# Gate products of a linear recurrence: from fp32 to three fp32r products of split parts, two halves later, with the weights asked for by ScalarE

## The reference, cut to what matters

```
xc = causal_dwconv(xb, lru_conv_w) + lru_conv_b            # xb, xc: 256 x 2048
xh = xc.reshape(1, 256, 8, 256)                            # 8 heads of 256 channels
r  = sigmoid(einsum("bshi,hij->bshj", xh, w_a) + b_a)      # w_a, w_x: 8 x 256 x 256
i  = sigmoid(einsum("bshi,hij->bshj", xh, w_x) + b_x)
log_a = -8 * r * softplus(-lam);  a = exp(log_a)
u  = xc * i * sqrt(-expm1(2 * log_a))
h_t = a_t * h_(t-1) + u_t                                  # over the tokens
y_b = h * silu(z_b)
```

## Time and profile before

| what | value |
|---|---|
| median of three runs | 2910.55 us |
| profiled execution, its time | 2911.19 us |
| profiled execution, its span | 2909.5 us |
| TensorE busy | 2871.9 us, 99% |
| VectorE busy | 1944.8 us, 67% |
| ScalarE busy | 1644.5 us, 57% |
| mean granted TensorE clock | 0.996 |
| DMA, mean over the span | 219 GB/s |

### The profile page before, as it was taken

One profiled execution on the slowest core, in us unless ns is written; L12 is line 12 of the kernel. 1 busy time (PEld: TensorE's weight loads), 2 busy tenths in 40 slices (PEclk: granted clock), 3 DMA queues, 4 the chain that ended last, 5 costly groups with the idle time before them and its releaser, 6 DMA issues.

```text
span 2909.5 us, 40342 instructions
## 1 busy us (share of the span) xinstructions
PE 2871.9 (99%) x16476; PEld 2532.0 (87%) x16476; DVE 1944.8 (67%) x2244; ACT 1644.5 (57%) x1912; POOL 98.6 (3%) x82
## 2 busy tenths in 40 slices
PE   8999999999899999999999999999999999999998
PEld 8989988898777878788999988888899999888886
DVE  6767444535699999999675864555565678555556
ACT  6554444534478878787555544555545654444544
POOL 2212000000000000000000000000000000000000
PEclk9999999999999999999999999999999999999999
DMA  7545566645389999999555555555564545655555
GB/s 268 186 159 170 185 213 237 208 159 175 133 330 352 360 360 358 358 361 325 174 174 174 187 182 192 182 190 174 190 199 148 200 163 181 201 188 185 186 196 188
DMA packets 282102, 636.66 MB, mean 219 GB/s; under 512 B 19081, under 2 KB 32962, under 8 KB 264642
## 3 DMA queue, kind: packets, MB, share of 16 engines
q1 hardware_dynamic: 280450, 628.86, 62.8%
q10 hardware_dynamic: 1184, 4.20, 0.4%
q0 software_dynamic: 288, 1.05, 0.1%
HBM read 626.72 MB, written 7.36 MB: 218 GB/s over the span
## 4 chain that ended last, share of the span: by engine, by line
PE 92%; DVE 4%; ACT 1%; issue 1%; DMA 0%; ACTq 0%; SPq 0%; POOL 0%; DVEq 0%; POOLq 0%
PE pairs L741 16%; PE pairs L743 16%; PE pairs L742 16%; PE pairs L761 10%; PE pairs L763 10%; PE pairs L765 10%; PE pairs L1118 3%; DVE w_lo L2087 2%; PE pairs L1119 2%; PE pairs L1120 2%; PE misc L1234 2%; ACT w_hi L1478 1%; PE misc L908 1%; DVE b_lo L2606 1%; PE misc L981 0%
## 5 line engine op out<-in xcount | busy, mean ns | idle before, releaser
L2087 DVE TENSOR_TENSOR w_lo<-raw,w_hi 128x1024 fp32r<-128x1024 f32 x1072 | 1307.8, 1239 | 800.4 <-ACT w_hi L1478 793.2
L1478 ACT ACTIVATE w_hi<-raw 128x1024 fp32r<-128x1024 f32 x1072 | 1120.5, 1059 | 940.3 <-PE pairs L743 543.7
L761 PE MATMUL pairs<-a_hi,w_hi 128*128 128x256 f32 x1920 | 549.2, 286 | 2.2 <-DVE w_lo L2087 2.2
L763 PE MATMUL pairs<-a_lo,w_hi 128*128 128x256 f32 x1920 | 544.2, 283 | 0.0
L765 PE MATMUL pairs<-a_hi,w_lo 128*128 128x256 f32 x1920 | 544.1, 283 | 0.0
L741 PE MATMUL pairs<-w_hi,a_hi 128*128 128x512 f32 x1280 | 504.5, 394 | 6.0 <-DVE w_lo L2087 3.1
L743 PE MATMUL pairs<-w_hi,a_lo 128*128 128x512 f32 x1280 | 498.5, 389 | 0.0
L742 PE MATMUL pairs<-w_lo,a_hi 128*128 128x512 f32 x1280 | 498.3, 389 | 0.0
L761 PEld LDWEIGHTS pairs<-a_hi,w_hi 128*128 128x128 f32 x1920 | 369.2, 192 | 4.3 <-issue 2.4
L763 PEld LDWEIGHTS pairs<-a_lo,w_hi 128*128 128x128 f32 x1920 | 369.4, 192 | 0.5
L765 PEld LDWEIGHTS pairs<-a_hi,w_lo 128*128 128x128 f32 x1920 | 369.2, 192 | 0.0
(11 more groups left out here) (387 smaller groups left out, 3038.0 us busy)
## 6 DMA issues: line engine op xcount, KB each, us to landing
raw<-in_w_in_dram SPq DMA_DIRECT2D x232, 1024.0 KB, 5.1
raw<-in_w_out_dram SPq DMA_DIRECT2D x84, 1024.0 KB, 5.1
raw<-in_w_down_dram SPq DMA_DIRECT2D x54, 1024.0 KB, 7.1
raw<-in_w_gate_dram SPq DMA_DIRECT2D x51, 1024.0 KB, 6.0
raw<-in_w_up_dram SPq DMA_DIRECT2D x51, 1024.0 KB, 6.6
raw<-in_xattn_wk_dram SPq DMA_DIRECT2D x16, 1024.0 KB, 5.0
raw<-in_xattn_wv_dram SPq DMA_DIRECT2D x16, 1024.0 KB, 5.0
raw<-in_xattn_wq_dram SPq DMA_DIRECT2D x16, 1024.0 KB, 5.0
```

The lines of the kernel that those rows point to most:

```text
L761: nc.tensor.matmul(o, w_hi[:, s, q, fs], hi[:, k, :], start=(k == 0 and f % 2 == 0), stop=False, skip_group_check=True)
L763: nc.tensor.matmul(o, w_hi[:, s, q, fs], lo[:, k, :], start=False, stop=False, skip_group_check=True)
L1478: a.activation(w_hi[:, h % HSLOTS], landing(h)[:, 2 * (h % 2):2 * (h % 2) + 2, :], ACT.Copy).then_inc(hi_done, 1)
L2087: v.tensor_tensor(w_lo[:, h % HSLOTS], landing(h)[:, 2 * (h % 2):2 * (h % 2) + 2, :], w_hi[:, h % HSLOTS].bitcast(F32), ALU.subtract).then ...
```

## The change

The gates are computed as the large products are: `w_ax` and `xc` are split in high and low parts and three fp32r products replace each fp32 one.

- The high part of the weights, `w_ax_hi`, lies in the place of `qm` (not in use then); the low part takes the place of `w_ax` itself. The parts of `xc` go to the last quarter of `b_hi` and `b_lo`.
- ScalarE: `gate_weights_hi(j)` (two copies of 128x1024) before h6 of unit 2j+1, `conv_hi(j)` (one copy) before h4 of unit 2j+2.
- VectorE: `gate_weights_lo(l, j)` (two subtractions of 128x1024) behind h7 of unit 2j+1, `conv_lo(l, j)` (one) before h5 of unit 2j+2.
- TensorE: the blocks stand behind h3 and h4 instead of h1 and h2, 24 products each, after a wait for both low parts.
- The weights of group 0 are still asked for by SP, those of groups 1 to 3 by ScalarE right behind the sigmoids of the group before; SP's three waits go.

```diff
--- before.py
+++ after.py
@@ -274,6 +274,9 @@
         Tb = sc(9232, 4, S)
         Zb = sc(10256, 4, S)
         w_ax = sc(11280, 2, 4, S)
+        w_ax_lo = rounded("w_ax_low", 11280, [P, 2, 4, S])
+        w_ax_hi = rounded("w_ax_high", 0, [P, 2, 4, S])
+        xc_hi, xc_lo = b_hi[:, 12:16, :], b_lo[:, 12:16, :]
         w_if = sc(13328, KT, 16)
         w_if_g = w_if.rearrange("p (q r) (g c) -> p g q r c", q=4, g=2)
         vx = sc(4096, TT, 2, S + 1)
@@ -441,6 +444,8 @@
         win_done = sem("win_done")
         xp_zero = sem("xp_zero")
         vx_ones = sem("vx_ones")
+        gate_hi = sem("gate_hi")
+        gate_lo = sem("gate_lo")
         landed.append(sem("landed_fifth"))
 
         def turn_bank(n):
@@ -682,10 +687,10 @@
                 for j in range(4):
                     units(H[f"lru{l}"] + 2 * j * HALVES, 1, w_in2[l], XB2 + j * COLS)
                     for c in range(CHUNKS):
-                        if c == 1:
-
-                            if l or j:
-                                sp.wait_ge(gates_mm, 4 * l + j)
+                        if c == 1 and j == 0:
+
+                            if l:
+                                sp.wait_ge(gates_mm, 4 * l)
                             for m, name in enumerate(("w_a_2", "w_x_2")):
                                 sp.dma_start(w_ax[:, m], t[name][l, 2 * j:2 * j + 2]
                                              .rearrange("h (k p) n -> p (h k) n", p=P))\
@@ -1224,16 +1229,18 @@
             def lru_gates(l, j, a):
 
                 g = 4 * l + j
-                pe.wait_ge(conv_ok, 8 * l + j + 1)
-                pe.wait_ge(wax_in, 32 * (g + 1))
+                pe.wait_ge(gate_lo, 2 * (g + 1))
                 if g:
                     pe.wait_ge(gates_ok, g)
                 for m_ in range(2):
                     for f in range(2):
+                        o = misc[:, 2 * m_ + a, f * S:(f + 1) * S]
                         for k in range(2):
-                            m = nc.tensor.matmul(misc[:, 2 * m_ + a, f * S:(f + 1) * S],
-                                                 w_ax[:, m_, 2 * a + k, f * P:(f + 1) * P],
-                                                 xc[:, 2 * a + k, :], start=k == 0, stop=k == 1)
+                            n = 2 * a + k
+                            h, z = (w[:, m_, n, f * P:(f + 1) * P] for w in (w_ax_hi, w_ax_lo))
+                            nc.tensor.matmul(o, h, xc_hi[:, n, :], start=k == 0, stop=False)
+                            nc.tensor.matmul(o, h, xc_lo[:, n, :], start=False, stop=False)
+                            m = nc.tensor.matmul(o, z, xc_hi[:, n, :], start=False, stop=k == 1)
                 if a:
                     m.then_inc(gates_mm, 1)
 
@@ -1320,13 +1327,13 @@
                         hooks = {1: lambda: rows_out(l)}
                     if n >= 2 and n % 2 == 0:
                         j = n // 2 - 1
-                        hooks = {1: (lambda j=j: lru_gates(l, j, 0)), 2: (lambda j=j: lru_gates(l, j, 1))}
+                        hooks = {3: (lambda j=j: lru_gates(l, j, 0)), 4: (lambda j=j: lru_gates(l, j, 1))}
                     unit(pc(U[f"lru{l}"] + n), H[f"lru{l}"] + n * HALVES, n % 2, mm_features, a_hi,
                          a_lo, need=ready(4 + l) if n == 0 else {}, hooks=hooks)
                 for n in range(4):
                     hooks = {}
                     if n == 0:
-                        hooks = {1: lambda: lru_gates(l, 3, 0), 2: lambda: lru_gates(l, 3, 1)}
+                        hooks = {3: lambda: lru_gates(l, 3, 0), 4: lambda: lru_gates(l, 3, 1)}
                     unit(pc(U[f"qk{l}"] + n), H[f"qk{l}"] + n * HALVES, n % 2, mm_features, a_hi,
                          a_lo, hooks=hooks)
                 for n in range(4):
@@ -1891,6 +1898,27 @@
                                              misc[:, b + k // 2, (k % 2) * S:(k % 2 + 1) * S],
                                              ACT.Sigmoid, bias=col(f"{name}{l}", 4 * j + k))
                     m.then_inc(gates_ok, 1)
+                    if j < 3:
+                        for m, name in enumerate(("w_a_2", "w_x_2")):
+                            act.dma_start(w_ax[:, m], t[name][l, 2 * j + 2:2 * j + 4]
+                                          .rearrange("h (k p) n -> p (h k) n", p=P)).then_inc(wax_in, 16)
+
+                def gate_weights_hi(j):
+
+                    n = 4 * l + j
+                    act.wait_ge(wax_in, 32 * (n + 1))
+                    act.wait_ge(spread, 4 * GROUPS)
+                    if n:
+                        act.wait_ge(gates_mm, n)
+                    if l:
+                        act.wait_ge(bc_mm, 4 * l)
+                    a.activation(w_ax_hi[:, 0], w_ax[:, 0], ACT.Copy)
+                    a.activation(w_ax_hi[:, 1], w_ax[:, 1], ACT.Copy).then_inc(gate_hi, 1)
+
+                def conv_hi(j):
+
+                    act.wait_ge(conv_ok, 8 * l + j + 1)
+                    a.activation(xc_hi, xc, ACT.Copy).then_inc(gate_hi, 1)
 
                 def exps(j):
                     act.wait_ge(gates_ok, 4 * l + j + 1)
@@ -1917,8 +1945,11 @@
                     a.activation(dst[:, 4 * (n % 2):4 * (n % 2) + 4, :], xc, ACT.Silu)\
                      .then_inc(qk_ok, 1)
 
+                if m_ <= 7 and m_ % 2 == 1:
+                    todo[6].append(lambda: gate_weights_hi(m_ // 2))
                 if 2 <= m_ <= 8 and m_ % 2 == 0:
                     j = m_ // 2 - 1
+                    todo[4].append(lambda: conv_hi(j))
                     todo[5].append(lambda: z_silu(j))
                     todo[8].append(lambda: sigmoids(j))
                 if 3 <= m_ <= 9 and m_ % 2 == 1:
@@ -2796,6 +2827,18 @@
                 if f == 3:
                     m.then_inc(conv_ok, 1)
 
+            def gate_weights_lo(l, j):
+
+                dve.wait_ge(gate_hi, 2 * (4 * l + j) + 1)
+                for i in range(2):
+                    m = v.tensor_tensor(w_ax_lo[:, i], w_ax[:, i], w_ax_hi[:, i].bitcast(F32), ALU.subtract)
+                m.then_inc(gate_lo, 1)
+
+            def conv_lo(l, j):
+
+                dve.wait_ge(gate_hi, 2 * (4 * l + j) + 2)
+                v.tensor_tensor(xc_lo, xc, xc_hi.bitcast(F32), ALU.subtract).then_inc(gate_lo, 1)
+
             def one_minus_a2(l, j):
 
                 dve.wait_ge(a2_ok, 4 * l + j + 1)
@@ -2974,6 +3017,9 @@
                         todo[2].append(lambda i=i: conv_tile(l, i, 3))
                     if 2 <= m_ <= 8 and m_ % 2 == 0:
                         todo[3].append(lambda: z_in(l, m_ // 2 - 1))
+                        todo[5].append(lambda: conv_lo(l, m_ // 2 - 1))
+                    if m_ <= 7 and m_ % 2 == 1:
+                        todo[8].append(lambda: gate_weights_lo(l, m_ // 2))
                     if m_ == 12:
                         todo[6].append(lambda: gate_rows(l))
                     if 3 <= m_ <= 9 and m_ % 2 == 1:
```

## The result

| kernel | median us | ratio to before, 95% interval |
|---|---|---|
| before | 2911.11 (7 runs) | |
| after | 2919.89 (2919.44 to 2921.10, 7 runs) | 1.0029 (1.0020 to 1.0039) |

The change costs 8.8 us. In the profiled executions the spans stand 9.1 us apart (2918.6 against 2909.5); 0.6 of it lies before the first product of the LRU units (1365.21 against 1364.59 us), and belongs to none of the prediction's terms.

The account below looks back on a forecast made before the run. TensorE, busy 99% of the span, was taken to bound the kernel. Terms -9.1 + 4.1 + 2.7 + 14.0 + 0.4 = +12.1 us gave 2923.3 us profiled, 2922.7 us on the median; range 2906 to 2934 us.

Parts of the forecast that it names:

- The gate products: TensorE's 16 gate blocks: each takes 2.88 us as fp32r products instead of 3.45 us, -9.1 us in all.
- the old stall: TensorE's existing 0.22 us wait at h1 of odd units, once per group; its removal counted as -1.8 us.
- Stall S: h1 of odd units: later gates make TensorE wait for ScalarE behind the sigmoids, 0.73 us per group, net +4.1 us.
- The table load hidden: ScalarE's sigmoids: the 1.28 us table load runs before the wait for the gates, costing nothing; otherwise +10.2 us.
- The issues on ScalarE: Weight transfers issued behind the sigmoids, six pairs at 0.45 us: +2.7 us, with bounds 0 and +5.4.
- Stall D: Even units of groups 1 to 3: VectorE's weight subtractions make h0 to h2 late, 2.34 us six times, +14.0 us.
- The splits on ScalarE: ScalarE's high-part copies before h6 of odd and h4 of even units: hidden, no cost; uncovered, 3 us a group.
- First group: Layer 0, first group: VectorE's added subtractions make the gates start late, +0.4 us, once.
- Rival (a): TensorE never waits, decided at h2 of even units: -10.9 us, 2899.7 us; chance 0.09.

Follow-up runs that it names:

- e9: Kernel after with weight subtractions moved before h4 of even units, exponentials one half later, and `y_lo` and `z_in` of groups 1 to 3 behind the subtractions: 2900.1 us.
- e2: Kernel after with both VectorE subtractions for the low gate weights left out, the low products reading the high part: 2906.6 us.
- e7: Kernel after with the gate blocks back behind h1 and h2 and both convolution parts made as soon as it is there: 2915.5 us.
- e4: Kernel after with the two waits before ScalarE's sigmoids in the other order, the late one (gates) written second: 2930.9 us.
- e10: Kernel after with SP asking for the gate weights of all groups again, with its waits, instead of ScalarE: 2919.1 us.
- e1: Kernel after with one of the two VectorE subtractions per group for the low gate weights left out: 2912.8 us.
- e5: Kernel after with VectorE's two gate-weight subtractions moved from behind h7 of the odd unit to before h4 of the even unit: 2906.9 us.
- e3: Kernel after with ScalarE's exponentials one half later, behind the high half of h1 instead of before it: 2915.2 us.
- e8: Kernel after with the two gate-weight subtractions on GpSimd instead of VectorE: 2936.3 us.

## Why the prediction was right, point by point

Forecast +12.1 us, measured +8.8 (spans +9.1).

- **The gate products, -9.1.** Right. e9, with nothing waiting, stands at -11.4 us, where -9.1 for the products and -1.8 for the old stall were forecast. A block is 2.83 us rather than 2.88, so the products' gain was 9.9 us; the 0.8 more in 16 blocks covers the 0.5 between the two.
- **Stall S, +4.1.** Right. e2 shows 0.73 us alone. e7 brings it back to the old 0.22 us (spacings of 0.24 and 0.22 where two of 0.12 are usual, in each of the 8 groups) and gains 4.4 us; 0.51 x 8 = 4.1 was forecast.
- **The table load hidden.** Right, and for the reason given: e4 reverses the order of the waits and pays 11.0 us (forecast 10.2; 1.34 us a group instead of 1.28).
- **The issues on ScalarE, +2.7.** This is the term that was mis-sized, and most of the 3.3 us between forecast and measurement: they cost nothing that can be seen. They are issued from 0.03 us after the first sigmoid's start, while the others run, and from there to the next high half takes the same 2.86 or 2.87 us; e10 agrees within 0.8 us. My bounds held this end, but I took the middle between an issue that had stood alone between two activations and none. That row was of another situation: there the transfer had to wait for the activation's result. The issue itself, 0.37 to 1.41 us here, was not too small to matter; it was covered.
- **Stall D, +14.0.** Right in place, cause and nearly in size: 13.2 us by e1 and e2 together, with 0.4 of it the first group's. In the trace it comes to 2.27 us in the even unit of group 1 against the forecast 2.34, with three short restarts where the forecast had one, and h2's low half ends 28.10 us after h1's start (forecast 28.11).
- **The splits on ScalarE, 0.** Right: e2 has them all and no wait in the even units.
- **First group, +0.4.** Right: one start 0.50 us behind the product before it instead of 0.12, and 0.10 for the restart.

Without the issues' 2.7 the sum would have been +9.4 us, against 9.1 in the spans. That it lies so near is in part luck: 0.6 of the 9.1 lies ahead of the LRU units, and the products gave 0.8 more than forecast. Rival (a), no wait at all, names what the change could have been (e9), and failed where it was said to: at h2 of the even units.

The two halves' delay, which I had priced only by S, was not tested against its alternative in the prediction. e7 shows that it is a small loss by itself (4.4 us), and e9 that with it the whole gain can be had: the place in which e5 and e9 put the two subtractions, behind the low half of h3, lies ahead of the gates only because these come two halves later. Whether another order of VectorE's row would reach e9's time without the delay was not run.

## What to carry to other kernels

Utilisation says little about room. Here an engine that was idle a third of the time charged nearly every microsecond put into its queue, since it came into the one stretch in which the engine had no gap and, with the gate block moved away, a margin of 0.08 us; a few instructions later the same work was free. Before adding or moving work, walk that engine's queue from its last idle gap to each release the bottleneck wants, and write both times side by side; when the bottleneck's own filler is moved (the gate blocks here), redo it for what stood behind the filler. And what is gained at the head of such a row counts only as far as its end moves too (e3).

## What the runs showed of the hardware that was not expected

- GpSimd beside VectorE: two subtractions of 128x1024 on GpSimd stretched four scans from 2.44 to 6.75 us, and giving the two subtractions to the idle engine cost 16.4 us more than leaving them with the busy one (e8).
- Of six waits of 2.9 us (e8) four were followed by a stretch below full clock, down to 0.50 over 6 us, and two by none; of eight starts 2.09 us behind the product before (e4) four were, and lost nothing net by it; the waits of up to 1.2 us in after were not (1.00 from 1440 to 1650 us).
- Of two waits before an activation that needs a table load, the first written stayed on the activation and the second stood before the load, in both orders tried: 1.28 us on or off the path (e4).
- Transfers on ScalarE's queue were issued while activations written before them were still to run: at 1434.36, 0.03 us after the first of eight sigmoids, though written behind the last, and not while that first one was still waiting.
